# Layer norm of the depthwise convolution: two passes over the tiles, or one with shifted sums

## The chip, the cores and the metric

The kernel runs on one core of one Trainium2 chip, all in one program. The time is the device time of an execution in microseconds (us); less is better.

## The reference, cut to what matters

The whole is a chain of residual blocks on a sequence of 256 tokens with 1024 features, in f32: a first part (mixer, cross attention, MLP), then a conformer convolution, a gated MLP, sparse attention and another gated MLP. The change lies in the convolution block alone:

```python
def layernorm(x, g, b):
    xf = x.astype(jnp.float32)
    mu = jnp.mean(xf, axis=-1, keepdims=True)
    var = jnp.mean(jnp.square(xf - mu), axis=-1, keepdims=True)
    y = (xf - mu) * lax.rsqrt(var + EPS_2)
    return (y * g.astype(jnp.float32) + b.astype(jnp.float32)).astype(x.dtype)

def conformer_conv(h, w_pw1, b_pw1, w_dw, b_dw, ln_g, ln_b, w_pw2, b_pw2):
    u = h @ w_pw1 + b_pw1
    a, gate = jnp.split(u, 2, axis=-1)
    u = a * jax.nn.sigmoid(gate)
    u = causal_dwconv_2(u, w_dw, b_dw)        # 31 taps for each channel
    u = jax.nn.silu(layernorm(u, ln_g, ln_b))
    return u @ w_pw2 + b_pw2
```

The norm is over the 1024 channels of each token.

## The kernel before, in words

All activations lie feature-major: a tile is 128 channels (partitions) by 256 tokens, and there are eight. The weights come as a stream of 512 KB chunks, loaded by SyncE's DMA queue into the ring `WR`, and are split in two for three products (high by high, high by low, low by high; lines L867 to L869): ScalarE makes the high half `WH` (L1232), VectorE the low half `WL` (L1477). Each engine has its program in its own order, fixed by hand; `sp.to(n)` puts the split of the chunks up to n at that place of an engine's program, and the engines meet at semaphores. `AHEAD` is 3 chunks.

The first matrix `pw1` has 16 output tiles, gates and values by turns. VectorE scales each (L1492), ScalarE applies the sigmoid (L1406), and VectorE multiplies the two into the padded tile `UPAD` (L1807). Then comes the depthwise convolution, two tiles at a time in four rounds p = 0 to 3. Of its 31 taps VectorE does 13 as partial sums in `CD` (`taps` on VectorE, L1823 to L1828) and TensorE 18, as products with diagonal matrices of 64 by 64 that GpSimd builds in `DG` (L1974); the results stand in PSUM (`big`). TensorE's `taps(p)` runs the 18 (L1164), waits for `part_done`, and adds `CD` through the identity (L1169). A round is followed on ScalarE by `conv_out(p)`, a copy of the two tiles to `CX` (L1398).

TensorE's order is: tiles of `pw1` 0 to 7, then `taps(0)`, tiles 8 to 11, `taps(1)`, feature sums of `CX` 0 and 1, tiles 12 to 15, `taps(2)`, sums 2 and 3, `taps(3)`, sums 4 to 7. A sum over features is a matmul with a matrix of ones in plain f32 (L1175), which leaves the sum in all partitions. VectorE turns it into the mean `MU` (L1854) and subtracts this from the eight tiles (L1856); ScalarE squares each (L1415), TensorE sums the squares (`sum_squares("ln")`, L875), ScalarE takes Ln and Exp to have 1/sqrt (L1249, L1250), VectorE multiplies (L1859), ScalarE applies Silu with gain and bias (L1419) and rounds the high half `YH` (L1422), GpSimd the low half `YL` (L1936). The next matrix `pw2` begins with all three.

A function of ScalarE needs a table that holds it, and a change of table is an instruction of its own; `preload_act_table_set` puts one at a chosen place (L1412).

Of the kernel before, what the change touches and what calls it, by code (L numbers as in the profile page):

```python
# [7 lines left out]
P = 128  # L8
T = 256
TT = T // P  # L10
D = 1024
KD = D // P
# [15 lines left out]
F32 = mybir.dt.float32  # L28
F32R = mybir.dt.float32r
ALU = mybir.AluOpType  # L30
ACT = mybir.ActivationFunctionType
# [66 lines left out]
def program(nc, x_d, mem_d, stream_d, vec_d, const_d, small_d, out_d):  # L98
    stack = ExitStack()
    with stack:  # L100
# [5 lines left out]
        def sem(name):  # L106
            if name not in sems:
                sems[name] = stack.enter_context(nc.semaphore(name))
            return sems[name]
# [5 lines left out]
        SQ = sb("SQ", [P, KD, T])  # L115
# [7 lines left out]
        LNV = sb("LNV", [P, T])  # L123
        RS = sb("RS", [P, T])
        RS2 = sb("RS2", [P, T])
        SSUM = sb("SSUM", [P, T])
        ONES = sb("ONES", [P, P])
        EPS = sb("EPS", [P, 2])
        RST = sb("RST", [P, TT])

        def group(specs):
# [31 lines left out]
        OS = QT  # L163

        B = group([("SG", [P, 2, T], F32), ("AT", [P, 2, T], F32), ("UP", [P, KD, T + CONV_W - 1], F32),
                   ("CX", [P, KD, T], F32), ("CD", [P, 2, 2, 2, T], F32), ("MU", [P, T], F32),
                   ("DG", [P, 2, PE_TAPS, 2, 64], F32)])
        SG, AT, UPAD, CX, CD, MU, DG = (B[n] for n in ("SG", "AT", "UP", "CX", "CD", "MU", "DG"))
        C = group([("GU", [P, 2, T], F32), ("UH", [P, 2, T], F32R), ("UL", [P, 2, T], F32R),
# [16 lines left out]
        big = stack.enter_context(nc.psum_tensor("big", [P, 4, 512], F32))  # L186
        mis = stack.enter_context(nc.psum_tensor("mis", [P, 2, 512], F32))
# [12 lines left out]
        def con(name, a=0, b=None):  # L200
            w = dict(CONSTS)[name]
            return CON[:, CCOL[name] + a:CCOL[name] + (w if b is None else b)]
# [22 lines left out]
        class Chain:  # L225
# [15 lines left out]
            def link(self, ins):  # L241
                self.eng.wait_ge(self.sem, self.add(ins))
# [614 lines left out]
        def _(pe):  # L857
# [22 lines left out]
            def sum_squares(name):  # L880
                for k in range(SQ_COUNT.get(name, 8)):
                    sum_square(name, k)
# [271 lines left out]
            def taps(p):  # L1154


                pe.wait_ge(sem("up_ready"), 2 * p + 2)
                pe.wait_ge(sem("diagonals"), p + 1)
                if p >= 2:
                    pe.wait_ge(sem("cx_whole"), 2 * p - 2)  # L1160
                halves = [(r, c, slice(64 * r, 64 * r + 64), slice(64 * c, 64 * c + 64)) for r in range(2) for c in range(2)]
                for i in range(PE_TAPS):
                    for r, c, rs, cs in halves:
                        pe.matmul(big[cs, 2 * (p % 2) + r, 0:T], DG[rs, p % 2, i, c, :], UPAD[rs, 2 * p + c, i:i + T],  # L1164
                                  start=i == 0, stop=False, skip_group_check=True)
                pe.wait_ge(sem("part_done"), 4 * p + 4)
                for a in range(2):
                    for r, c, rs, cs in halves:
                        ins = pe.matmul(big[cs, 2 * (p % 2) + r, 0:T], con("ident2")[rs], CD[rs, p % 2, c, a],  # L1169
                                        start=False, stop=a == 1, skip_group_check=True)  # L1170
                ins.then_inc(sem("taps_ps"), 1)

            def sum_features(j):
                pe.wait_ge(sem("cx_whole"), j + 1)
                return pe.matmul(mis[:, 1, 0:T], ONES[:, :], CX[:, j], start=j == 0, stop=j == KD - 1,  # L1175
                                 skip_group_check=True)

# [2 lines left out]
            for p in range(4):  # L1180
                if p < 3:
                    gated(2 * p + 2)
                    gated(2 * p + 3)
                taps(p)
                if p >= 1:
                    sum_features(2 * p - 2)
                    sum_features(2 * p - 1)
            sum_features(KD - 2)
            sum_features(KD - 1).then_inc(sem("mean_ps"), 1)
            sum_squares("ln")  # L1190
            for j in range(KD):
                tile(START["pw2"] + j, TILE["pw2"] + j, YH, YL, base=(yl_ready, Y_BASE["pw2"]) if j == 0 else None)

# [29 lines left out]
        def _(act):  # L1223
# [22 lines left out]
            def rstd(name, out):  # L1246
                act.wait_ge(nps_ready, NORM[name] + 1)
                e = EPS[:, int(NORM[name] > NORM["final"]):int(NORM[name] > NORM["final"]) + 1]
                link(act.activation(LNV[:, :], mis[:, 0, 0:T], ACT.Ln, bias=e, scale=1.0 / NORM_DIM.get(name, D)))  # L1249
                act.activation(out[:, :], LNV[:, :], ACT.Exp, scale=-0.5).then_inc(rstd_ready, 1)  # L1250
# [143 lines left out]

            def conv_out(p):
                act.wait_ge(sem("taps_ps"), p + 1)
                for r in range(2):
                    act.activation(CX[:, 2 * p + r], big[:, 2 * (p % 2) + r, 0:T], ACT.Copy).then_inc(sem("cx_whole"), 1)  # L1398

            C0 = START["pw1"]  # L1400
            sp.to(C0 + 1 + AHEAD)
# [1 line left out]
            for j in range(8):  # L1403
                sp.to(C0 + 2 * j + 1 + AHEAD)
                act.wait_ge(acc_free, TILE["pw1"] + 2 * j + 1)
                act.activation(SG[:, j % 2], SG[:, j % 2], ACT.Sigmoid,  # L1406
                               bias=vec("b_pw1", 2 * j)).then_inc(sem("gate_done"), 1)
                sp.to(C0 + 2 * j + 2 + AHEAD)
                if j % 2 == 1 and j >= 3:
                    conv_out((j - 3) // 2)  # L1410
            conv_out(3)
            act.preload_act_table_set("natural_log_exp_and_others")  # L1412
            for k in range(KD):
                act.wait_ge(sem("cx_centred"), k + 1)
                act.activation(SQ[:, k], CX[:, k], ACT.Square).then_inc(sq_ready, 1)  # L1415
            rstd("ln", RS2)
            for k in range(KD):
                act.wait_ge(gy_ready, GY_BASE["pw2"] + k + 1)
                silu = ch.add(act.activation(GY[:, k], GY[:, k], ACT.Silu, bias=vec("ln_b", k), scale=vec("ln_g", k)))  # L1419
# [50 lines left out]
        def _(dve):  # L1470
# [342 lines left out]
            def taps(p, first, stop):  # L1813

                for m in range(first, stop):
                    c, n = m // own, m % own
                    j, i = 2 * p + c, PE_TAPS + m % own
                    x, w, o = UPAD[:, j, i:i + T], vec("w_dw", CONV_W * j + i), CD[:, p % 2, c, n % 2]
                    if n == 0:
                        dve.wait_ge(sem("up_ready"), j + 1)  # L1820
                        if p >= 2:
                            dve.wait_ge(sem("taps_ps"), p - 1)
                        tapped[0] = ch.add(dve.tensor_scalar(o, x, w, vec("b_dw", j), ALU.mult, ALU.add))  # L1823
                    elif n == 1:
                        tapped[1] = ch.add(dve.tensor_scalar(o, x, w, None, ALU.mult))
                    else:
                        dve.wait_ge(dve_chain, tapped[n % 2])
                        ins = dve.scalar_tensor_tensor(o, x, w, o, ALU.mult, ALU.add)  # L1828
                        if n < own - 2:
                            tapped[n % 2] = ch.add(ins)  # L1830
                        else:
                            ins.then_inc(sem("part_done"), 1)

            for p in range(5):
                if p < 4:
                    gate_half(2 * p)
                if p >= 1:
                    taps(p - 1, 0, 3)
                if p < 4:
                    value_half(2 * p)  # L1840
                    gated(2 * p)
                if p >= 1:
                    taps(p - 1, 3, 6)
                if p < 4:
                    gate_half(2 * p + 1)
                if p >= 1:
                    taps(p - 1, 6, 9)
                if p < 4:
                    value_half(2 * p + 1)
                    gated(2 * p + 1)  # L1850
                if p >= 1:
                    taps(p - 1, 9, 2 * own)
            dve.wait_ge(sem("mean_ps"), 1)
            link(dve.tensor_scalar(MU[:, :], mis[:, 1, 0:T], 1.0 / D, None, ALU.mult))  # L1854
            for k in range(KD):
                dve.tensor_tensor(CX[:, k], CX[:, k], MU[:, :], ALU.subtract).then_inc(sem("cx_centred"), 1)  # L1856
            rstd_done("ln")
            for k in range(KD):
                dve.tensor_tensor(GY[:, k], CX[:, k], RS2[:, :], ALU.mult).then_inc(gy_ready, 1)  # L1859
            for j in range(KD):  # L1860
                used(START["pw2"] + j)
                t = TILE["pw2"] + j
                link(dve.scalar_tensor_tensor(X[:, j], acc[:, t % 2, 0:T], vec("b_pw2", j), X[:, j], ALU.add, ALU.add))
                dve.sem_inc(acc_free, 1)
                gx("ffn2_0", j)
                if j > 0:
                    add_square("ffn2_0", j - 1)
                sp.to(START["pw2"] + j + 1 + AHEAD)
# [276 lines left out]
```

## Time and profile before

| | |
|---|---|
| time, median of 3 runs | 1168.76 us (1169.74, 1165.75, 1168.76) |
| profiled execution, its own time | 1165.05 us |
| its span in the profile | 1163.2 us |
| granted TensorE clock, mean over the span | 0.977 of full speed |
| TensorE matmuls busy | 1088.1 us, 94% |
| VectorE busy | 786.2 us, 68% |
| ScalarE busy | 530.8 us, 46% |
| GpSimd busy | 166.4 us, 14% |

The span is the time between the first and the last instruction; what lies around it makes up the rest of the execution's time. Busy time is a sum over the span and says nothing of who waits for whom. In a timeline each row has a start, a length, an engine, a line of the kernel, the tile written and those read, how many instructions stand in the row (x), and in brackets how long the engine had been idle before it and what released it. PE is TensorE, PEld its weight load, DVE VectorE, ACT ScalarE, POOL GpSimd. A plain f32 matmul leaves two records. Matmuls overlap, so the length of one is more than its share of the time; the distance between starts is what it costs.

### The profile page before, as it was taken

What the parts mean: (1) busy time and instruction counts of PE and PEld (TensorE: products, weight loads), DVE (VectorE), ACT (ScalarE), POOL (GpSimd) and SP (SyncE); (2) the same over time, 40 slices, a digit from 0 to 9 for tenths busy, and PEclk for the clock granted to TensorE, in tenths of its full rate; (3) what the DMA queues carried; (4) which work ended last, traced back from release to release, by engine and by line L of the source; (5) the groups of instructions that cost most, each with busy time, mean ns of one, the idle gap of its engine ahead of it and who ended that gap; (6) DMA issues with size and microseconds to landing.
All of it is one profiled execution on the core that took longest, in us unless ns stands there. A gap on an engine that the chain in (4) does not pass through costs nothing.

```text
span 1163.2 us, 22985 instructions
## 1 busy us (share of the span) xinstructions
PE 1088.1 (94%) x8721; PEld 1030.3 (89%) x8721; DVE 786.2 (68%) x1314; ACT 530.8 (46%) x917; POOL 166.4 (14%) x180
## 2 busy tenths in 40 slices
PE   5999899889999989997999999988899999999997
PEld 4989569789999979776999999987888999999997
DVE  5866567575555568884777677658966657777675
ACT  5443265454444445126544444445535545444442
POOL 2020014031111115112310100120010021100100
PEclk9999799899999999998999999989999999999999
DMA  8553214256566643321456555553630025655551
GB/s 309 156 166 100 59 51 132 96 157 186 184 185 184 181 145 122 98 74 28 159 195 191 181 173 195 182 145 94 215 113 16 2 73 158 200 179 186 180 192 44
DMA packets 46437, 165.25 MB, mean 142 GB/s; under 512 B 5152, under 2 KB 6176, under 8 KB 46240
## 3 DMA queue, kind: packets, MB, share of 16 engines
q1 hardware_dynamic: 45216, 163.24, 44.4%
q10 hardware_dynamic: 1152, 1.05, 0.4%
q8 instruction: 49, 0.80, 0.3%
q14 instruction: 20, 0.16, 0.0%
HBM read 162.17 MB, written 1.05 MB: 140 GB/s over the span
## 4 chain that ended last, share of the span: by engine, by line
PE 77%; DVE 15%; ACT 4%; issue 2%; POOL 1%; DMA 1%; SPq 0%; DVEq 0%; ACTq 0%
PE acc L867 14%; PE acc L869 14%; PE acc L868 14%; PE big L867 6%; PE big L869 6%; PE big L868 6%; DVE WL L1477 4%; DVE CD L1828 2%; PE mis L875 2%; PE acc L471 2%; PE big L442 1%; DVE G L1484 1%; PE acc L928 1%; PE acc L930 1%; PE acc L929 1%
## 5 line engine op out<-in xcount | busy, mean ns | idle before, releaser
L1477 DVE TENSOR_TENSOR WL<-WR,WH 128x1024 fp32r<-128x1024 f32 x302 | 370.6, 1239 | 152.9 <-ACT WH L1232 142.8
L867 PE MATMUL acc<-XH,WH 128*128 128x256 f32 x1392 | 406.1, 292 | 29.7 <-DVE WL L1477 13.3
L869 PE MATMUL acc<-XH,WL 128*128 128x256 f32 x1392 | 396.7, 285 | 0.0
L868 PE MATMUL acc<-XL,WH 128*128 128x256 f32 x1392 | 396.4, 285 | 0.0
L1232 ACT ACTIVATE WH<-WR 128x1024 fp32r<-128x1024 f32 x302 | 313.3, 1051 | 130.1 <-PE acc L869 90.5
L867 PEld LDWEIGHTS acc<-XH,WH 128*128 128x128 f32 x1392 | 269.5, 194 | 35.5 <-issue 20.1
L868 PEld LDWEIGHTS acc<-XL,WH 128*128 128x128 f32 x1392 | 269.3, 193 | 1.1
L869 PEld LDWEIGHTS acc<-XH,WL 128*128 128x128 f32 x1392 | 269.0, 193 | 0.0
L867 PE MATMUL big<-UH,WH 128*128 128x256 f32 x608 | 170.6, 281 | 0.3 <-POOL UL L1940 0.3
L868 PE MATMUL big<-UL,WH 128*128 128x256 f32 x608 | 169.7, 279 | 0.0
L869 PE MATMUL big<-UH,WL 128*128 128x256 f32 x608 | 169.7, 279 | 0.0
L1940 POOL TENSOR_TENSOR UL<-GU,UH 128x256 fp32r<-128x256 f32 x76 | 56.3, 741 | 493.4 <-ACT UH L1367 493.4
L867 PEld LDWEIGHTS big<-UH,WH 128*128 128x128 f32 x608 | 114.5, 188 | 0.5 <-POOL UL L1940 0.5
L869 PEld LDWEIGHTS big<-UH,WL 128*128 128x128 f32 x608 | 114.3, 188 | 0.0
L868 PEld LDWEIGHTS big<-UL,WH 128*128 128x128 f32 x608 | 114.1, 188 | 0.0
L1367 ACT ACTIVATE UH<-GU 128x256 fp32r<-128x256 f32 x76 | 31.8, 418 | 160.8 <-DVE GU L1746 86.8
L1932 POOL TENSOR_TENSOR XL<-G,XH 128x256 fp32r<-128x256 f32 x56 | 63.0, 1137 | 186.2 <-ACT XH L1239 186.2
L867 PE MATMUL acc<-YH,WH 128*128 128x256 f32 x256 | 76.1, 297 | 7.8 <-POOL YL L1936 6.4
L868 PE MATMUL acc<-YL,WH 128*128 128x256 f32 x256 | 73.4, 287 | 0.0
L869 PE MATMUL acc<-YH,WL 128*128 128x256 f32 x256 | 73.3, 286 | 0.0
L867 PEld LDWEIGHTS acc<-YH,WH 128*128 128x128 f32 x256 | 50.0, 195 | 10.6 <-issue 5.4
L868 PEld LDWEIGHTS acc<-YL,WH 128*128 128x128 f32 x256 | 50.2, 196 | 0.1
(296 smaller groups left out, 1341.1 us busy)
## 6 DMA issues: line engine op xcount, KB each, us to landing
WR<-weights SPq DMA_DIRECT2D x302, 512.0 KB, 3.6
X<-x_t SPq DMA_DIRECT2D x4, 256.0 KB, 6.3
MEM<-mem_t SPq DMA_DIRECT2D x1, 1024.0 KB, 10.1
result_t<-X SPq DMA_DIRECT2D x4, 256.0 KB, 2.2
CON<-constants SPq DMA_DIRECT2D x1, 896.0 KB, 12.3
CBUF<-KCV ACTq DMA_DIRECT2D x4, 128.0 KB, 5.5
CBUF<-KCV ACTq DMA_DIRECT2D x4, 127.5 KB, 6.3
SML<-small_weights SPq DMA_DIRECT2D x1, 480.0 KB, 14.2
```

Source lines behind the costliest of these rows:

```text
L442: pe.matmul(o[:, P:P + T], QP[:, j, P:T], k, start=False, stop=True, skip_group_check=True)
L471: ins = pe.matmul(acc[:, 0, (2 * br + tt) * P:(2 * br + tt) * P + P], PT[:, hh % 2, br, b * P:b * P + P], NV[:, m, 128 * g + 64 * br:128 * ...
L867: pe.matmul(out, wh, hi, start=start, stop=False, skip_group_check=True)
L868: pe.matmul(out, wh, lo, start=False, stop=False, skip_group_check=True)
L869: return pe.matmul(out, wl, hi, start=False, stop=stop, skip_group_check=True)
L875: ins = pe.matmul(mis[:, 0, 0:T], ONES[:, :], SQ[:, k], start=k == 0, stop=k == n - 1, skip_group_check=True)
L1232: act.activation(WH[:, cs % SPL], WR[:, cs % RAW], ACT.Copy).then_inc(w_high, 1)
L1367: act.activation(UH[:, us % 2], GU[:, us % 2], ACT.Copy).then_inc(u_high, 1)
L1477: dve.tensor_tensor(WL[:, cs % SPL], WR[:, cs % RAW], WH[:, cs % SPL].bitcast(F32), ALU.subtract).then_inc(w_low, 1)
L1828: ins = dve.scalar_tensor_tensor(o, x, w, o, ALU.mult, ALU.add)
L1932: pool.tensor_tensor(XL[:, k], G[:, k], XH[:, k].bitcast(F32), ALU.subtract).then_inc(xl_ready, 1)
L1940: pool.tensor_tensor(UL[:, us % 2], GU[:, us % 2], UH[:, us % 2].bitcast(F32), ALU.subtract).then_inc(sem("u_low"), 1)
```

## The change

The mean of the first 256 channels (tiles 0 and 1), called the shift here, is taken as soon as round 0 is in `CX`. It is subtracted from tiles 0 and 1 by VectorE, and from tiles 2 to 7 by one more group of identity matmuls in PSUM. From then on TensorE sums both the values and their squares as tiles come, and the variance is the mean of the squares less the square of the mean. Squares are taken straight from PSUM. Tiles are centred on VectorE behind the statistics, three ahead and the rest between the scalings.

```diff
@@ tiles
-                   ("CX", [P, KD, T], F32), ("CD", [P, 2, 2, 2, T], F32), ("MU", [P, T], F32),
+                   ("CX", [P, KD, T], F32), ("CD", [P, 2, 2, 2, T], F32), ("MU", [P, 3, T], F32),
@@ TensorE, taps(p)
+                if p == 1:
+                    for j in range(2):
+                        pe.wait_ge(sem("cx_whole"), j + 1)
+                        ins = pe.matmul(mis[:, 1, T:2 * T], ONES[:, :], CX[:, j], start=j == 0, stop=j == 1,
+                                        skip_group_check=True)
+                    ins.then_inc(sem("shift_ps"), 1)
                 pe.wait_ge(sem("part_done"), 4 * p + 4)
-                for a in range(2):
+                if p == 1:
+                    pe.wait_ge(sem("shift_done"), 1)
+                for a in range(2 if p == 0 else 3):
                     for r, c, rs, cs in halves:
-                        ins = pe.matmul(big[cs, 2 * (p % 2) + r, 0:T], con("ident2")[rs], CD[rs, p % 2, c, a],
-                                        start=False, stop=a == 1, skip_group_check=True)
+                        x = CD[rs, p % 2, c, a] if a < 2 else MU[rs, 0]
+                        ins = pe.matmul(big[cs, 2 * (p % 2) + r, 0:T], con("ident2")[rs], x, start=False,
+                                        stop=a == (1 if p == 0 else 2), skip_group_check=True)
@@ TensorE, sum_features(j): waits for cx_shifted (j < 2), cx_whole (j < 6) or cx_last
@@ TensorE, behind taps(p)
-                if p >= 1:
-                    sum_features(2 * p - 2)
-                    sum_features(2 * p - 1)
+                if p >= 2:
+                    for j in (2 * p - 4, 2 * p - 3):
+                        sum_features(j)
+                        sum_square("ln", j)
+            for j in (4, 5):
+                sum_features(j)
+                sum_square("ln", j)
             sum_features(KD - 2)
             sum_features(KD - 1).then_inc(sem("mean_ps"), 1)
-            sum_squares("ln")
+            for n, k in ((7, KD - 1), (8, KD - 2)):
+                pe.wait_ge(sq_ready, SQ_BASE["ln"] + n)
+                ins = pe.matmul(mis[:, 0, 0:T], ONES[:, :], SQ[:, k], start=False, stop=n == 8, skip_group_check=True)
+            ins.then_inc(nps_ready, 1)
@@ ScalarE, conv_out(p)
-                for r in range(2):
-                    act.activation(CX[:, 2 * p + r], big[:, 2 * (p % 2) + r, 0:T], ACT.Copy).then_inc(sem("cx_whole"), 1)
+                for r in range(2) if p < 3 else (1, 0):
+                    if p < 3:
+                        act.activation(CX[:, 2 * p + r], big[:, 2 * (p % 2) + r, 0:T], ACT.Copy).then_inc(sem("cx_whole"), 1)
+                    elif r == 0:
+                        act.wait_ge(sem("cx_last"), 1)
+                    if p > 0:
+                        act.activation(SQ[:, 2 * p + r], big[:, 2 * (p % 2) + r, 0:T], ACT.Square).then_inc(sq_ready, 1)
@@ ScalarE, in the loop over the gates, ahead of conv_out(1), and behind it
+                if j == 5:
+                    for r in range(2):
+                        act.wait_ge(sem("cx_shifted"), r + 1)
+                        act.activation(SQ[:, r], CX[:, r], ACT.Square).then_inc(sq_ready, 1)
...
+            act.preload_act_table_set("natural_log_exp_and_others")
             conv_out(3)
-            act.preload_act_table_set("natural_log_exp_and_others")
-            for k in range(KD):
-                act.wait_ge(sem("cx_centred"), k + 1)
-                act.activation(SQ[:, k], CX[:, k], ACT.Square).then_inc(sq_ready, 1)
-            rstd("ln", RS2)
+            act.wait_ge(sem("var_done"), 1)
+            link(act.activation(LNV[:, :], MU[:, 2], ACT.Ln, bias=EPS[:, 1:2]))
+            act.activation(RS2[:, :], LNV[:, :], ACT.Exp, scale=-0.5).then_inc(rstd_ready, 1)
@@ VectorE, behind its taps of round 1
+                if p == 2:
+                    dve.wait_ge(sem("shift_ps"), 1)
+                    dve.tensor_scalar(MU[:, 0], mis[:, 1, T:2 * T], -1.0 / (2 * P), None,
+                                      ALU.mult).then_inc(sem("shift_done"), 1)
+                    dve.wait_ge(sem("shift_done"), 1)
+                    for j in range(2):
+                        dve.tensor_tensor(CX[:, j], CX[:, j], MU[:, 0], ALU.add).then_inc(sem("cx_shifted"), 1)
@@ VectorE, behind all taps
+            dve.wait_ge(sem("taps_ps"), 4)
+            for r in range(2):
+                if r == 1:
+                    dve.wait_ge(sq_ready, SQ_BASE["ln"] + 7)
+                dve.tensor_copy(CX[:, 6 + r], big[:, 2 + r, 0:T]).then_inc(sem("cx_last"), 1)
             dve.wait_ge(sem("mean_ps"), 1)
-            link(dve.tensor_scalar(MU[:, :], mis[:, 1, 0:T], 1.0 / D, None, ALU.mult))
-            for k in range(KD):
-                dve.tensor_tensor(CX[:, k], CX[:, k], MU[:, :], ALU.subtract).then_inc(sem("cx_centred"), 1)
+            link(dve.tensor_scalar(MU[:, 1], mis[:, 1, 0:T], 1.0 / D, None, ALU.mult))
+            link(dve.tensor_tensor(MU[:, 0], MU[:, 1], MU[:, 1], ALU.mult))
+            dve.wait_ge(nps_ready, NORM["ln"] + 1)
+            dve.scalar_tensor_tensor(MU[:, 2], mis[:, 0, 0:T], 1.0 / D, MU[:, 0], ALU.mult,
+                                     ALU.subtract).then_inc(sem("var_done"), 1)
+            def centred(k):
...
+                return ch.add(dve.tensor_tensor(CX[:, k], CX[:, k], MU[:, 1], ALU.subtract))
+            left = [centred(k) for k in range(3)]
             rstd_done("ln")
             for k in range(KD):
+                dve.wait_ge(dve_chain, left[k])
                 dve.tensor_tensor(GY[:, k], CX[:, k], RS2[:, :], ALU.mult).then_inc(gy_ready, 1)
+                if k + 3 < KD:
+                    left.append(centred(k + 3))
```

## Rows read from the trace of the kernel before

**Rows 1.** The page, part 4: shares of the chain of waits.

```profile
PE 77%; DVE 15%; ACT 4%; issue 2%; POOL 1%; DMA 1%; SPq 0%; DVEq 0%; ACTq 0%
```

**Rows 2.** Timeline of TensorE, 494 to 535 us: start, length, engine, line.

```profile
494.28 1.09 PE L1169 MATMUL big<-CD,CON 64*64 64x256 f32 x16 [1.13 <-DVE CD L1828]
495.30 1.13 PE L1175 MATMUL mis<-CX,ONES 128*128 128x256 f32 x4
...
516.42 1.09 PE L1169 MATMUL big<-CD,CON 64*64 64x256 f32 x16 [0.54 <-DVE CD L1828]
...
518.50 8.01 PE L1164 MATMUL big<-UP,DG 64*64 64x256 f32 x144
...
526.29 0.64 PEld L1169 LDWEIGHTS big<-CD,CON 64*64 64x64 f32 x16 [0.25 <-DVE CD L1828]
...
527.32 1.99 PE L1175 MATMUL mis<-CX,ONES 128*128 128x256 f32 x8
530.74 3.72 PE L875 MATMUL mis<-SQ,ONES 128*128 128x256 f32 x16 [1.43 <-ACT SQ L1415]
```

**Rows 3.** Timeline of VectorE, 489 to 546 us.

```profile
489.79 4.43 DVE L1828 SCALAR_TENSOR_TENSOR CD<-UP,VEC,CD 128x256 f32<-128x256 f32 x11
499.35 0.42 DVE L1492 TENSOR_TENSOR SG<-acc,RS 128x256 f32<-128x256 f32 x1 [5.12 <-PE acc L869]
499.69 1.22 DVE L1477 TENSOR_TENSOR WL<-WR,WH 128x1024 fp32r<-128x1024 f32 x1
...
529.35 0.42 DVE L1854 TENSOR_SCALAR MU<-mis 128x256 f32<-128x256 f32 x1 [3.11 <-PE mis L1175]
529.81 2.77 DVE L1856 TENSOR_TENSOR CX<-CX,MU 128x256 f32<-128x256 f32 x8
...
545.13 0.48 DVE L1863 SCALAR_TENSOR_TENSOR X<-acc,VEC,X 128x256 f32<-128x256 f32 x1 [6.91 <-PE acc L869]
```

**Rows 4.** Timeline of ScalarE, 495 to 547 us.

```profile
495.44 0.66 ACT L1398 ACTIVATE CX<-big 128x256 f32<-128x256 f32 x2 [10.56 <-PE big L1169]
495.98 1.06 ACT L1232 ACTIVATE WH<-WR 128x1024 fp32r<-128x1024 f32 x1
...
534.50 0.47 ACT L1249 ACTIVATE LNV<-mis,EPS 128x256 f32<-128x256 f32 x1 [1.47 <-PE mis L875]
...
535.44 1.28 ACT L1419 ACT_TABLE_LOAD   x1
...
546.48 0.40 ACT L1240 ACTIVATE SQ<-X 128x256 f32<-128x256 f32 x1
```

**Rows 5.** Timeline of GpSimd (POOL), 495 to 545 us.

```profile
495.49 4.21 POOL L1974 TENSOR_TENSOR DG<-CON,VEC 128x1152 f32<-128x1152 f32 x2 [17.67 <-PE big L1169]
...
538.21 6.21 POOL L1936 TENSOR_TENSOR YL<-GY,YH 128x256 fp32r<-128x256 f32 x8 [38.52 <-ACT YH L1422]
```

**Rows 6.** Timeline of TensorE, the first products of `pw2`.

```profile
539.08 0.55 PE L867 MATMUL acc<-YH,WH 128*128 128x256 f32 x1 [4.62 <-POOL YL L1936]
...
540.17 0.42 PE L868 MATMUL acc<-YL,WH 128*128 128x256 f32 x1
540.39 0.41 PE L869 MATMUL acc<-YH,WL 128*128 128x256 f32 x1
...
544.70 0.28 PE L868 MATMUL acc<-YL,WH 128*128 128x256 f32 x1
544.82 0.28 PE L869 MATMUL acc<-YH,WL 128*128 128x256 f32 x1
```

**Rows 7.** Busy time by stretch; the third column from the end is the granted clock.

```profile
537.00:538.00 1.00, 0.00 (x0) 0.00 (x0) 1.00 (x4) 1.00 (x3) 0.00 (x0) 0.50 0.00 0
...
543.00:544.00 1.00, 1.00 (x5) 0.92 (x5) 0.00 (x0) 1.00 (x2) 1.00 (x2) 0.62 0.00 0
...
779.00:780.00 1.00, 1.00 (x8) 1.00 (x8) 0.00 (x0) 0.72 (x1) 0.00 (x0) 0.64 1.00 284
...
786.00:787.00 1.00, 1.00 (x10) 1.00 (x10) 1.00 (x2) 0.62 (x2) 0.00 (x0) 0.95 0.06 16
```

More of the change, by code:

```diff
@@ L1165, in taps @@
                                   start=i == 0, stop=False, skip_group_check=True)
+                if p == 1:
[4 more added lines that the diff above has]
+                    ins.then_inc(sem("shift_ps"), 1)
                 pe.wait_ge(sem("part_done"), 4 * p + 4)
-                for a in range(2):
+                if p == 1:
+                    pe.wait_ge(sem("shift_done"), 1)
+                for a in range(2 if p == 0 else 3):
                     for r, c, rs, cs in halves:
-                        ins = pe.matmul(big[cs, 2 * (p % 2) + r, 0:T], con("ident2")[rs], CD[rs, p % 2, c, a],
-                                        start=False, stop=a == 1, skip_group_check=True)
+                        x = CD[rs, p % 2, c, a] if a < 2 else MU[rs, 0]
+                        ins = pe.matmul(big[cs, 2 * (p % 2) + r, 0:T], con("ident2")[rs], x, start=False,
+                                        stop=a == (1 if p == 0 else 2), skip_group_check=True)
                 ins.then_inc(sem("taps_ps"), 1)
             def sum_features(j):
-                pe.wait_ge(sem("cx_whole"), j + 1)
+                if j < 2:
+                    pe.wait_ge(sem("cx_shifted"), j + 1)
+                elif j < 6:
+                    pe.wait_ge(sem("cx_whole"), j + 1)
+                else:
+                    pe.wait_ge(sem("cx_last"), j - 5)
                 return pe.matmul(mis[:, 1, 0:T], ONES[:, :], CX[:, j], start=j == 0, stop=j == KD - 1,
@@ L1852, in _ @@
                     taps(p - 1, 9, 2 * own)
-            dve.wait_ge(sem("mean_ps"), 1)
-            link(dve.tensor_scalar(MU[:, :], mis[:, 1, 0:T], 1.0 / D, None, ALU.mult))
-            for k in range(KD):
-                dve.tensor_tensor(CX[:, k], CX[:, k], MU[:, :], ALU.subtract).then_inc(sem("cx_centred"), 1)
+                if p == 2:
[10 more added lines that the diff above has]
+                dve.tensor_copy(CX[:, 6 + r], big[:, 2 + r, 0:T]).then_inc(sem("cx_last"), 1)
+            dve.wait_ge(sem("mean_ps"), 1)
+            link(dve.tensor_scalar(MU[:, 1], mis[:, 1, 0:T], 1.0 / D, None, ALU.mult))
[4 more added lines that the diff above has]
+            def centred(k):
+                if k < 6:
+                    dve.wait_ge(sem("cx_whole"), k + 1)
+                return ch.add(dve.tensor_tensor(CX[:, k], CX[:, k], MU[:, 1], ALU.subtract))
+            left = [centred(k) for k in range(3)]
             rstd_done("ln")
             for k in range(KD):
+                dve.wait_ge(dve_chain, left[k])
                 dve.tensor_tensor(GY[:, k], CX[:, k], RS2[:, :], ALU.mult).then_inc(gy_ready, 1)
+                if k + 3 < KD:
+                    left.append(centred(k + 3))
             for j in range(KD):
```

## The prediction

> **What bounds the kernel now.** I read the page first. 77% of the chain of waits is TensorE work [rows 1]: whatever adds TensorE time where TensorE sets the pace costs its full length, and whatever lands where another engine sets it costs nothing. The change touches only the convolution stage, some 457 to 545 us. There I read each engine's timeline, to see who is last at every hand-over.
>
> Call the four rounds p = 0 to 3. Each runs 144 small matmul records over the taps, then 16 that add VectorE's partial sums through an identity (L1169), which wait for VectorE. In round 1 TensorE stands 1.13 us before those [rows 2] and VectorE then idles 5.12 us until the next tile [rows 3]: slack on both sides, TensorE's at 493.2 to 494.3, VectorE's at 494.2 to 499.35. In round 2 TensorE waits again (0.54 us), so the start at 516.42 is VectorE's. In round 3 it doesn't wait; only its weight load does, for 0.25 us [rows 2]. So from 517.4 on TensorE is the pace, with at most 0.25 us of slack.
>
> Then the norm. TensorE sums the features to 529.31, VectorE makes the mean (0.42) and centres the first tile, ScalarE squares it, TensorE starts the squares at 530.74 and ends them at 534.46 [rows 2, 3, 4]. Ln starts at 534.50, the table load for Silu behind it runs from 535.44 to 536.72, and from there ScalarE and POOL pace all: Silu and high half of a tile, and POOL's low halves behind them in 6.21 us for 8, 0.78 a tile, to 544.42 [rows 4, 5]. The first product of the next matrix restarts at 539.08 and is fed at that pace [rows 6]. From 527.32 to the first Silu at 536.72, 9.4 us pass; that is all that this change can shorten, and ScalarE's part of it (from 534.50, 2.22 us) stays.
>
> **The change, part by part.**
>
> *Round 1 (shift).* Two more fp32 matmuls on TensorE between the taps and the identity adds. The taps end 1.13 before the adds' start at 494.28, at 493.15; two such matmuls take 1.13 (L1175 x4) [rows 2], so they end at 494.28, when VectorE's last tap (489.79 + 4.43 = 494.22) is also done. VectorE then writes the shift (as L1854, 0.42) to about 494.75 [rows 3], and TensorE's identity adds, which stand behind that wait with the weights product behind them, start at 494.8: 0.5 late. A third group of identity adds follows. One group is the half of 1.02 us (494.28 to 495.30) less the fill; I take 0.43, between 0.2 and 0.5. Taken away are two feature sums, 0.86 to 1.06. Sum: +0.5 +0.43 -0.86 = about +0.1 at the next tile, hence +0.1 for VectorE's restart at 499.35 and the whole of its unbroken work until 516.3. VectorE's two shifting adds (2 x 0.35, the pitch of L1856: 2.77 / 8) lie in its 5.12 us of idle time. ScalarE's squares of tiles 0 and 1 wait for them inside its 10.56 us of idle time before 495.44; the two squares among the copies put its next weight split (495.98) back by 0.9 for the later hand-over and 0.6 for the squares, to end near 498.6, while VectorE takes it at 499.69 [rows 3, 4]. That cover of about 1.1 us is the thinnest of the change: if it went, each 1 us over would go on VectorE's path. SP's queue and POOL's diagonals (4.21 us, from 496.4 to 500.6 instead of 495.49 to 499.7, wanted at 518.5) [rows 5] are not pushed past anything.
>
> *Round 2.* The identity adds start at 516.5. Third group +0.43. Then four sums stand where two stood. Four in a row take 1.99, two 1.13, so one more is 0.43; the eight squares in 3.72 give (3.72 - 1.99) / 4 = 0.43 as well [rows 2]. +0.86. The taps of round 3 start at 518.50 + 0.1 + 0.43 + 0.86 = 519.9, +1.4.
>
> *Round 3.* TensorE was at most 0.25 ahead of VectorE there; I take 0.15 as swallowed. Third group +0.43. The convolution is whole at 527.32 + 1.4 - 0.15 + 0.43 = 529.0, +1.7. ScalarE and VectorE then evacuate and square two tiles in turns (three or four steps of about 0.42, to 530.5), beside eight sums of older tiles (3.5 us, to 532.5): hidden. The table load moved ahead of this evacuation lies in the time in which ScalarE waits for round 3 (VectorE's and TensorE's work from 518.50 on): nothing.
>
> *The end of the sums.* Before, from 527.32: four sums, then mean, centring, first square (1.43 us of TensorE idle), eight sums, Ln at 534.50, that is 7.18 us. After: twelve sums without a break, 12 x 0.4325 + 0.3 = 5.49, to 534.5. The mean's own branch is as long: ten sums end at 529.0 + 4.33 + 0.3 = 533.6, mean 0.46, its square 0.46, 534.55. Then one new link, the variance on VectorE reading PSUM (0.48, L1863 [rows 3]) and a hand-over of 0.04: Ln at 535.1. Change: -1.7 for the gap and its hand-overs, +0.5 for the variance, so the +1.7 ends as +0.6.
>
> *Behind it.* Exp and the table load follow as before, so Silu starts at 537.35. VectorE now centres three tiles first (535.1 to 536.2), then alternates one scaled and one centred tile, 0.70 a pair: its first result is there at 536.65 under the table load, the second at 537.35, and from there it gives one per 0.70 against the 0.78 of ScalarE and POOL. Hidden, by 0.08 us a tile. The chain through POOL keeps its length. Net +0.6 us.
>
> **Ends of the unknown costs.** If the three identity groups cost only 0.2 each: -0.7, so -0.1. If each of the sums in a series that alternates between two output banks costs what a first one does (1.13 / 2 = 0.57, not 0.43): +0.14 x 14 = +2.0, so +2.6. I take the middle rows, since a row of eight in the same engine mode exists and the alternation has none: +0.6. The sum against the profiled execution is 1165.05 + 0.6 = 1165.7 (its span 1163.2 becomes 1163.8). But that execution is the fastest of the four shown; the runs beside it give 1165.75 to 1169.74, median 1168.76. I forecast the median: 1168.76 + 0.6 = 1169.4. This kernel's measurement can hardly tell less than 0.3%, 3.5 us, from no change.
>
> **Rivals.**
> 1. *A real gain.* The added sums and groups cost nothing before 529, because they fall where the taps are paced by VectorE. Then the convolution is whole at 527.4, sums end at 532.9, Ln at 533.5: -1.0, time 1167.8. For it: TensorE's weight load did wait for VectorE in round 3. Against it: for 0.25 us only, while 1.7 us are added. To gain over 3.5 us, more than a third of the 9.4 would have to vanish, and 5.5 of it are twelve sums. Chance 0.12.
> 2. *ScalarE's cover breaks in round 1 (or 2).* The added waits and squares hold the weight split back, VectorE idles, and its unbroken run to 516.3 moves. From the point where the split ends after 499.69, which is 1.1 us more than I count. A table load for a square between sigmoids (1.28 each way) would do it: 2.56 + 0.6 - 1.1 = +2.1, time 1170.9. Against it: under Silu's set the squares L1240 ran with no load between (546.48 after the load at 535.44) [rows 4]. Chance 0.10.
> 3. *Slower: the clock.* TensorE stood from 534.46 to 539.08 and its granted clock fell to 0.50 from about 537 to 543.4, that is from the 2.4 GHz level to 1.2 [rows 7]. It cost little, since ScalarE and POOL fed it at 0.78 a step. At the low level one matmul follows another by 0.22 us (540.17 to 540.39), at the high one by 0.12 (544.70 to 544.82) [rows 6], so a tile of 24 costs 2.4 us more. The standstill becomes 534.6 to 539.7, 0.5 longer. If the clock came back only 6.4 us behind the feed's end at 545, some 29 matmuls would be dear: 29 x 0.10 = 2.9, with +0.6 that is +3.5, time 1172.3 or more. That is the point from which it decides. For it: the same trace has a stretch with the engine busy throughout in which the clock was low from 779.6 to 786.05 [rows 7], some 6.4 us. Against it: behind the stand at 534 it came back 4.3 us after the restart, inside the fed tile. Chance 0.06.
>
> The Trainium skill, page "TensorE: Matmul & The Clock Gate", section "HAM oscillation — how this bites in real kernels", states that long pauses of the engine throttle its clock and that it has to be busy again before the clock is given back. By that rule this pause, being longer still, brings a dip in the changed kernel too. Here the trace agrees for the pause of 4.62 us [rows 6, 7]; the low stretch from 779.6, with the engine busy, is one that the rule doesn't explain.
>
> **How the numbers follow.** My forecast, -0.1 to +2.6, holds 0.68; rivals 0.12, 0.10 and 0.06; 0.04 for what I haven't seen. The runs of one kernel differ by 4 us here (a dip like that at 779.6 costs half its length, 3.2, and could be what comes and goes), so each case is blurred by about 2. Low end 1165.7: a median that catches the fast runs, 1165.75. High end 1172.2: the forecast with +2.6, and a slow draw, almost to rival 3. Faster by over 0.3%: 0.08, all of it from rival 1 and the draw. Slower by over 0.3%: 0.10, from rival 3 and half of the blur on rival 2. Within: 0.82.
>
> **What would show it.** Right: in the profile after, VectorE's restart near 499.4; round 3's taps start near 519.9; the identity adds of rounds 1 to 3 as 24 records, about 1.5 us each; twelve sums in a row in 5.5 us; Ln near 535.1; Silu near 537.4; the first matmul of the next matrix at 539.7. Wrong: the round 3 taps at 518.6 (rival 1); VectorE idle after 499.7 on a weight split, or a table load between sigmoids (rival 2); a granted clock of 0.50 past 546 (rival 3); sums with a pitch of more than 0.5 us, or VectorE late for a Silu.

## The result, and the profile after

The changed kernel takes 1170.74 us in the median of 22 runs (1163.97 to 1172.4); the kernel before, run beside it, 1167.24 us (22 runs, 1164.71 to 1170.13). The ratio is 1.0026, 95% interval 1.0015 to 1.0036: slower by 3.0 us, with 1.8 to 4.2 us as the bounds (the two medians as such lie 3.5 us apart). Forecast were 1169.4 us and +0.6 us over before.

Profiled executions wander by several us elsewhere, so I count inside one stretch, from ScalarE's first copy of round 0 (473.57 us before, 474.63 after: 1.06 of offset that the change has no part in) to VectorE's first residual (its first row `X<-acc` behind `pw2`). That length is called the stage here.

TensorE in the changed kernel, timeline, to hold against [rows 2] and [rows 6]:

```profile
494.14 1.13 PE L1170 MATMUL mis<-CX,ONES 128*128 128x256 f32 x4
495.88 1.09 PE L1179 MATMUL big<-CD,CON 64*64 64x256 f32 x16 [0.61 <-DVE MU L1886]
496.76 0.64 PE L1179 MATMUL big<-MU,CON 64*64 64x256 f32 x8
...
518.17 1.09 PE L1179 MATMUL big<-CD,CON 64*64 64x256 f32 x16 [1.13 <-DVE CD L1859]
...
521.55 8.00 PE L1164 MATMUL big<-UP,DG 64*64 64x256 f32 x144
529.38 1.04 PE L1179 MATMUL big<-CD,CON 64*64 64x256 f32 x16
530.24 0.61 PE L1179 MATMUL big<-MU,CON 64*64 64x256 f32 x8
530.78 0.70 PE L1190 MATMUL mis<-CX,ONES 128*128 128x256 f32 x2
...
535.20 1.03 PE L1212 MATMUL mis<-SQ,ONES 128*128 128x256 f32 x4
...
542.97 0.55 PE L867 MATMUL acc<-YH,WH 128*128 128x256 f32 x1 [6.74 <-POOL YL L1992]
```

The third identity group is the row of 8 records, 0.54 us from start to start in round 3 (530.24 to 530.78) with the refill behind it. The gap of 1.43 us in [rows 2] is gone, but the standstill ahead of the next matrix has grown from 4.62 to 6.74 us.

VectorE and ScalarE in the same kernel, against [rows 3] and [rows 4]:

```profile
495.31 0.42 DVE L1886 TENSOR_SCALAR MU<-mis 128x256 f32<-128x256 f32 x1
...
500.51 0.43 DVE L1523 TENSOR_TENSOR SG<-acc,RS 128x256 f32<-128x256 f32 x1 [3.98 <-PE acc L869]
500.85 1.95 DVE L1508 TENSOR_TENSOR WL<-WR,WH 128x1024 fp32r<-128x1024 f32 x1
...
541.15 1.09 DVE L1913 TENSOR_TENSOR GY<-CX,RS 128x256 f32<-128x256 f32 x3
548.67 0.48 DVE L1919 SCALAR_TENSOR_TENSOR X<-acc,VEC,X 128x256 f32<-128x256 f32 x1 [6.42 <-PE acc L869]
```

```profile
498.53 1.08 ACT L1255 ACTIVATE WH<-WR 128x1024 fp32r<-128x1024 f32 x1
...
536.80 0.51 ACT L1446 ACTIVATE LNV<-MU,EPS 128x256 f32<-128x256 f32 x1 [5.04 <-DVE MU L1901]
...
537.78 1.28 ACT L1450 ACT_TABLE_LOAD   x1
```

GpSimd, against [rows 5]; the last row is the first low half alone:

```profile
497.51 4.21 POOL L2030 TENSOR_TENSOR DG<-CON,VEC 128x1152 f32<-128x1152 f32 x2 [18.62 <-PE big L1179]
...
540.55 7.12 POOL L1992 TENSOR_TENSOR YL<-GY,YH 128x256 fp32r<-128x256 f32 x8 [38.84 <-ACT YH L1453]
...
540.55 2.28 POOL L1992 TENSOR_TENSOR YL<-GY,YH 128x256 fp32r<-128x256 f32 x1 [38.84 <-ACT YH L1453]
```

Two numbers stand out. The weight split at 500.85 takes 1.95 us, where its counterpart at 499.69 took 1.22, though its high half was ready (498.53 + 1.08). It ends at 502.80, 1.08 us after GpSimd's diagonals do (497.51 + 4.21 = 501.72). Before, the diagonals had ended at 499.70 (495.49 + 4.21) and the split began at 499.69: the two only just missed each other. And the first low half takes 2.28 us, where the eight took 6.21 together before: it starts at 540.55 amid VectorE's scalings and centrings and ends at 542.83, 0.59 us behind the last of them (541.15 + 1.09 = 542.24). Of its own work it has 0.73.

All kernels of this study, in us from the first copy of round 0 to the start of ScalarE's Ln, of its first Silu and of the first residual; ratios are to the kernel before:

| kernel | Ln | first Silu | first residual | time ratio (95%) |
|---|---|---|---|---|
| before | 60.93 | 63.16 | 71.56 | |
| changed | 62.17 | 64.44 | 74.04 | 1.0026 (1.0015 to 1.0036) |
| e1 | 62.34 | 64.61 | 73.99 | one execution |
| e2 | 62.18 | 64.45 | 73.22 | one execution |
| e3 (from before) | 62.06 | 64.29 | 72.70 | one execution |
| e4 | 62.18 | 64.45 | 73.76 | one execution |
| e5 | 59.34 | 61.61 | 70.92 | 0.9985 (0.9973 to 0.9997) |
| e6 | 58.74 | 61.01 | 69.49 | 0.9981 (0.9968 to 0.9994) |
| e7 (from before) | 60.33 | 62.57 | 70.61 | 1.0005 (0.9995 to 1.0016) |
| e8 | 58.75 | 61.02 | 68.74 | 0.9962 (0.9947 to 0.9977) |
| e9 | 62.18 | 64.46 | 72.93 | one execution |
| e10 (from before) | 60.34 | 62.57 | 70.30 | 0.9998 (0.9988 to 1.0008) |

Lengths up to Ln repeat well, so that one execution can be read to some hundredths of a us there: the four kernels with the same code up to Ln (changed, e2, e4, e9) have it at 62.17 or 62.18, e6 and e8 at 58.74 and 58.75, e7 and e10 at 60.33 and 60.34.

### The profile page after: what moved, and what is told of

It is laid out like the page before. It is cut to its first block, busy times and chain, and to the rows that moved or that the text cites. A ratio compares the mean times of both kernels' runs of the same rounds, so it can differ in the third digit from the quotient of the medians.

```text
span 1170.2 us, 23049 instructions
## 1 busy us (share of the span) xinstructions
PE 1092.6 (93%) x8749; PEld 1035.3 (88%) x8749; DVE 790.2 (68%) x1321; ACT 530.4 (45%) x915; POOL 167.8 (14%) x180
## 4 chain that ended last, share of the span: by engine, by line
PE 76%; DVE 16%; ACT 3%; issue 2%; POOL 1%; DMA 1%; SPq 0%; DVEq 0%; ACTq 0%
PE acc L867 14%; PE acc L869 14%; PE acc L868 14%; PE big L867 6%; PE big L869 6%; PE big L868 6%; DVE WL L1508 4%; DVE CD L1859 2%; PE mis L875 2%; PE acc L471 2%; PE big L442 1%; PE acc L928 1%; PE acc L929 1%; PE acc L930 1%; DVE G L1515 1%
```

## Experiments

**e1: diagonals earlier.**

```diff
+                ins.then_inc(sem("diag_read"), 1)      # TensorE, last product of the round with DG
-                    pool.wait_ge(sem("taps_ps"), p - 1)
+                    pool.wait_ge(sem("diag_read"), p - 1)
```

> The changed kernel, but GpSimd starts the diagonals of a round when TensorE's last product with the old ones has ended, and not when the whole round has. Stage length is counted from the first ScalarE copy of round 0 to the first residual on VectorE: 71.56 us before, 74.04 us changed. Theory (GpSimd and VectorE hold each other up when both read SBUF): the diagonals then end before VectorE splits its next weights, the split behind round 1's scaling takes 1.2 us and not 1.95, likewise the one behind round 0's (1.95 in both kernels), round 2's identity adds start 0.7 earlier, the stage is 0.7 to 1.5 us shorter (72.6 to 73.3). Rival (the split was long because ScalarE's high half or the load came late): both splits keep their 1.95 us and the stage its 74.0.

Measured: both splits short, the stage 73.99. The splits came as the theory had them, the gain did not. VectorE, ScalarE and GpSimd of this kernel show why:

```profile
477.01 1.21 DVE L1509 TENSOR_TENSOR WL<-WR,WH 128x1024 fp32r<-128x1024 f32 x1
...
494.31 0.42 DVE L1887 TENSOR_SCALAR MU<-mis 128x256 f32<-128x256 f32 x1 [0.62 <-PE mis L1171]
494.77 3.45 DVE L1891 TENSOR_TENSOR CX<-CX,MU 128x256 f32<-128x256 f32 x2
...
500.74 1.23 DVE L1509 TENSOR_TENSOR WL<-WR,WH 128x1024 fp32r<-128x1024 f32 x1 [0.80 <-ACT WH L1256]
```

```profile
498.25 0.42 ACT L1441 ACTIVATE SQ<-CX 128x256 f32<-128x256 f32 x1 [1.85 <-DVE CX L1891]
...
499.63 1.08 ACT L1256 ACTIVATE WH<-WR 128x1024 fp32r<-128x1024 f32 x1
```

```profile
493.32 4.61 POOL L2031 TENSOR_TENSOR DG<-CON,VEC 128x1152 f32<-128x1152 f32 x2 [16.84 <-PE big L1164]
```

The two shift additions on VectorE take 3.45 us instead of 0.76: they now stand inside GpSimd's work. ScalarE's square waits for them, its weight split comes late, and VectorE idles 0.80 us where the split had been 0.73 too long. What round 0's shorter split gained is already lost ahead of that: VectorE waits 0.62 us for TensorE's sum of the shift, and its first scaling of the next tile starts 25.87 us after the first copy (499.51), against 25.88 in the changed kernel. The collision moved; that is my second rival's chain (ScalarE's cover breaks), set off by GpSimd.

**e2: centring of tiles 3 to 7 left out** (part of the norm is not computed). The wait for those centrings goes too; the cut shows the work alone.

```diff
-                if k + 3 < KD:
-                    left.append(centred(k + 3))
```

> The changed kernel without the centring of tiles 3 to 7 (left out, so part of the norm is not computed): VectorE does eight scalings in a row and is done 1.7 us sooner. Theory: GpSimd's first low half, 2.28 us long in the changed kernel, takes 0.73 again, the first product of the next matrix starts 1.5 us earlier (about 4.0 us after the first Silu's start is 2.4 instead), and the stage is 1 to 2 us shorter than 74.04. Rival (the long first low half is GpSimd's own start, or the Silu chain is late because VectorE's alternation feeds it late): first low half stays above 1.5 us, stage within 0.3 of 74.0.

Measured: stage 73.22, 0.82 shorter; all eight low halves in 6.20 us, as before the change, while Silu starts where it did:

```profile
538.37 6.20 POOL L1990 TENSOR_TENSOR YL<-GY,YH 128x256 fp32r<-128x256 f32 x8 [38.84 <-ACT YH L1453]
```

The gain lies just under the 1 to 2 us expected. The first product stands 2.34 us after the first Silu, as in the kernel before (2.35), but the first residual 8.77 against 8.40. The 0.37 that are left go with the clock: it was granted at 0.50 until past 545.6, the end of the tile, where in the kernel before it rose inside the tile [rows 7].

**e3: the kernel before, diagonals later.**

```diff
-                    pool.wait_ge(sem("taps_ps"), p - 1)
+                    pool.wait_ge(sem("cx_whole"), 2 * (p - 1))
```

> The kernel before, with GpSimd's diagonals started only after ScalarE's two copies of the round, some 0.65 us later than before. Theory: now they overlap the weight split at 499.7 (1.22 us before), which grows to 1.7 to 1.95 us, and round 2's identity adds start 0.5 to 0.7 later; stage 71.56 + 0.6 = 72.1. Rival: the split keeps 1.22 us and the stage 71.56, since nobody waits for the diagonals.

Measured: 72.70, +1.14. GpSimd and VectorE in it:

```profile
475.44 4.20 POOL L1974 TENSOR_TENSOR DG<-CON,VEC 128x1152 f32<-128x1152 f32 x2 [21.94 <-ACT CX L1398]
...
498.00 4.20 POOL L1974 TENSOR_TENSOR DG<-CON,VEC 128x1152 f32<-128x1152 f32 x2 [18.36 <-ACT CX L1398]
```

```profile
478.08 2.64 DVE L1477 TENSOR_TENSOR WL<-WR,WH 128x1024 fp32r<-128x1024 f32 x1
...
501.51 1.77 DVE L1477 TENSOR_TENSOR WL<-WR,WH 128x1024 fp32r<-128x1024 f32 x1
```

Round 0 in the trace of the kernel before, GpSimd and VectorE:

```profile
473.62 4.20 POOL L1974 TENSOR_TENSOR DG<-CON,VEC 128x1152 f32<-128x1152 f32 x2 [21.24 <-PE big L1169]
```

```profile
476.95 1.95 DVE L1477 TENSOR_TENSOR WL<-WR,WH 128x1024 fp32r<-128x1024 f32 x1
```

Nobody waits for the diagonals, and still 0.69 us of delay in each round costs all of it in round 0 and 0.55 in round 1: round 1's split grows from 1.22 to 1.77, and round 0's, which had collided all along (1.95), to 2.64. I had counted round 1 alone. Each split ends 1.08 us after GpSimd's diagonals: at 503.28 behind 502.20, and at 480.72 behind 479.64.

**e4: the standstill filled.**

```diff
+            for i in range(12):
+                pe.matmul(big[:, i % 2, 0:T], ONES[:, :], SQ[:, 0], start=True, stop=True, skip_group_check=True)
```

> The changed kernel with twelve more fp32 matmuls of the size of a sum (into free PSUM, never read) behind the last sum of squares, so that TensorE works for 5.2 us of its 6.7 us standstill. If the clock is part of the loss: granted clock 1.00 throughout, the eight steps of the next matrix's first tile run at 0.36 us and are bound by GpSimd's low halves, the first residual comes 0.3 to 0.6 us earlier, stage 73.5 to 73.7. Rival (the clock costs nothing, since the feed is slower than TensorE at either level): stage 74.0, or longer if the fill holds the first product up.

Measured: 73.76, -0.28. By stretches (the granted clock is the third column from the end), the changed kernel first, then e4:

```profile
544.00:546.00 2.00, 2.00 (x10) 2.00 (x10) 0.00 (x0) 2.00 (x6) 2.00 (x4) 0.50 0.00 0
546.00:548.00 2.00, 2.00 (x10) 2.00 (x10) 0.00 (x0) 0.52 (x1) 1.67 (x3) 0.50 0.00 0
```

```profile
543.00:545.00 2.00, 1.86 (x10) 1.24 (x11) 0.00 (x0) 2.00 (x6) 2.00 (x4) 1.00 0.00 0
545.00:547.00 2.00, 1.78 (x10) 1.17 (x10) 0.00 (x0) 1.39 (x3) 2.00 (x4) 1.00 0.00 0
```

The clock stays at 2.4 GHz and the steps still come 0.69 us apart, at the rate of GpSimd's low halves. So in the changed kernel the clock is worth 0.3 us, no more: the low clock and GpSimd's pace are limits of nearly the same size.

**e5: the single pass without the shift.** The shift's matmuls, the third identity groups, VectorE's three shift instructions and the wait go; in their place:

```diff
                 if p == 1:
...
+                    for j in range(2):
+                        sum_features(j)
+                        sum_square("ln", j)
...
-                if p == 1:
-                    pe.wait_ge(sem("shift_done"), 1)
-                for a in range(2 if p == 0 else 3):
+                for a in range(2):
```

> The changed kernel without the shift: sums and squares are of the convolution as it is; the shift's two matmuls, the third identity group of rounds 1 to 3, VectorE's three shift instructions and the wait for them go, and the four sums of tiles 0 and 1 run in round 1 ahead of the identity adds. Stage (first copy of round 0 to first residual) 71.56 us before, 74.04 changed. Theory (the shift costs three groups of 0.43 and a wait of 0.5, and the single pass by itself saves the 1.43 us gap and two hand-overs): Ln comes 58.6 to 59.4 us after the first copy (60.93 before, 62.17 changed), the first Silu 2.3 later; GpSimd's long first low half stays, so the stage is 70.3 to 71.0 and the time 0.2% below before. Rival (the added length is the sums' own, alternating between two banks): Ln stays above 61, stage above 73.

Measured: 70.92, 3.12 shorter than the changed kernel; Ln at 59.34. In TensorE's timeline the four sums stand in round 1, where both kernels have it wait for VectorE, and the identity adds follow with no row for a wait:

```profile
493.65 0.59 PE L1182 MATMUL mis<-CX,ONES 128*128 128x256 f32 x2
494.08 0.59 PE L875 MATMUL mis<-SQ,ONES 128*128 128x256 f32 x2
494.61 1.10 PE L1173 MATMUL big<-CD,CON 64*64 64x256 f32 x16
```

The rival falls: sums that alternate between two banks start 0.43 us apart here too (493.65 to 494.08), and Ln is far below 61. The time, 0.9985, is 0.15% below before where 0.2% was expected. The first low half still takes 2.28 us in this kernel.

**e6: as e5, and GpSimd and VectorE apart.** The edit of e1, and VectorE does the low halves; GpSimd's are removed.

```diff
+            def low_half(k):
+                dve.wait_ge(yh_ready, Y_BASE["pw2"] + k + 1)
+                dve.tensor_tensor(YL[:, k], GY[:, k], YH[:, k].bitcast(F32), ALU.subtract).then_inc(yl_ready, 1)
...
+                if k >= 5:
+                    low_half(k - 5)
+            for k in range(3, KD):
+                low_half(k)
```

> As e5, with GpSimd and VectorE kept apart: the diagonals start when TensorE's last product with the old ones has ended (VectorE has no two-input work then, since the shift is gone), and VectorE takes the low halves of the eight tiles itself, behind its scalings, so that GpSimd has nothing there. Theory: no weight split of 1.95 us in the stage (0.7 less in each of rounds 0 and 1), Ln at 57.8 to 58.8 after the first copy, the first product of the next matrix 2.6 us after the first Silu, the last low half 7.0 after it; stage 69.0 to 70.0, bound in its last part by TensorE at the low clock. Time 0.2% to 0.4% below before. Rival (keeping them apart only moves the waits, as in e1): stage as in e5 within 0.3.

Measured: 69.49; no long split is left, Ln 0.60 earlier than in e5. The last part is bound by TensorE at the low clock, as expected: in this stretch it is busy throughout at a granted clock of 0.50, and VectorE and GpSimd are idle:

```profile
543.00:544.00 1.00, 1.00 (x6) 1.00 (x6) 0.00 (x0) 0.42 (x1) 0.00 (x0) 0.50 0.00 0
```

**e7: the kernel before, with the same two edits.**

> The kernel before (two passes), with GpSimd and VectorE kept apart in the same two places. Theory: the weight split behind round 0 takes 1.2 and not 1.95 us, everything from there to Silu comes 0.7 earlier (Ln at 60.2 after the first copy), the low halves on VectorE save another 0.3: stage 70.4 to 70.9 against 71.56, time 0.1% below before. If e7 gains as much as e6, the single pass gives nothing; if e6 is 1 us or more shorter in the stage, that is the single pass's own worth. Rival (no contention at all in the kernel before): 71.56.

Measured: 70.61, 0.95 shorter than before; the split behind round 0 takes 1.22 again:

```profile
476.67 1.22 DVE L1478 TENSOR_TENSOR WL<-WR,WH 128x1024 fp32r<-128x1024 f32 x1
```

The time doesn't show it: 1.0005, interval 0.9995 to 1.0016, where 0.9992 would be 0.95 us and lies outside the interval. Why is open (below). Against e6 the single pass without a shift is worth 1.12 us in the stage and 1.6 up to Ln.

**e8: e6 with the twelve filling matmuls.**

> As e6, with the twelve filling matmuls behind the last sum of squares. Theory (in e6 the first tile of the next matrix is bound by TensorE at its low clock, 0.695 us a step): with the clock at 1.00 the tile is bound by ScalarE's high halves, 0.80 a step from an earlier start, and the stage is 0.5 to 1.2 us shorter than e6's. Rival (ScalarE's pace hides the clock): same stage as e6 within 0.3.

Measured: 68.74, 0.75 less than e6; ratio 0.9962. TensorE and VectorE:

```profile
531.53 5.34 PE L1208 MATMUL big<-SQ,ONES 128*128 128x256 f32 x24
537.52 0.36 PE L867 MATMUL acc<-YH,WH 128*128 128x256 f32 x1 [0.65 <-DVE YL L1895]
...
540.44 0.39 PE L867 MATMUL acc<-YH,WH 128*128 128x256 f32 x1 [0.18 <-DVE YL L1895]
...
541.24 0.39 PE L867 MATMUL acc<-YH,WH 128*128 128x256 f32 x1 [0.18 <-DVE YL L1895]
```

```profile
542.26 0.48 DVE L1911 SCALAR_TENSOR_TENSOR X<-acc,VEC,X 128x256 f32<-128x256 f32 x1 [0.73 <-PE acc L869]
```

TensorE now waits 0.18 us for each of the last two low halves, which come 0.80 us apart, as ScalarE's high halves do (539.53, 540.33): the end of the stage is bound by ScalarE's pace. This version beats the kernel before, and by its ratio the changed one too.

**e9: the changed kernel, complete, low halves on VectorE** (e6's edit of the low halves alone).

> The changed kernel, complete, with the eight low halves ahead of the next matrix taken by VectorE behind its scalings and none by GpSimd; the diagonals and the shift stay. Theory (in the changed kernel GpSimd's first low half waited for VectorE's burst): Ln and Silu as in the changed kernel (62.2 and 64.4 after the first copy of round 0), the first product about 3.2 us after the first Silu instead of 3.9, the first residual 8.5 after it instead of 9.6; stage 72.9 to 73.2. Rival (only GpSimd's own rate of 0.73 a tile is in question and ScalarE is ahead of it anyway): stage within 0.3 of 74.0.

Measured: 72.93, 1.11 shorter, with Ln and Silu where they were. The first product stands 2.98 us after the first Silu, against 3.90. The rest of the gain lies behind it, where the steps come 0.64 us apart instead of 0.69:

```profile
541.12 0.55 PE L867 MATMUL acc<-YH,WH 128*128 128x256 f32 x1 [5.83 <-DVE YL L1911]
```

**e10: the kernel before with all of e8 but the single pass.**

> The kernel before (two passes) with all that e8 has beside the single pass: diagonals started early, low halves on VectorE, twelve filling matmuls behind the sum of squares. Theory (the single pass without the shift is worth 1.5 us of e8's 2.8 in the stage: Ln 60.33 in e7, 58.75 in e8): Ln at 60.3, stage 70.1 to 70.4, time between before and e8, about 0.1% below before. Rival (e8 gains by the clock alone): stage within 0.4 of e8's 68.74, time as e8's.

Measured: 70.30, time 0.9998 (0.9988 to 1.0008), where about 0.1% less was expected. The single pass without the shift is worth 1.56 us in the stage, all of it ahead of Silu: from the first Silu to the first residual e8 takes 7.72 us and e10 7.73. The filling matmuls are a little too many here. The first product follows them without a wait, 2.56 us after the first Silu and not 2.00 as in e7; TensorE makes that up before the tile ends. The intervals of e8 and e10 don't touch, so the gain in time is real; their quotient, 0.9964, is some 4 us with an uncertainty of 2, more than the stage shows (below).

## Why the prediction was right, and where it was short

The time lay in the range and within 0.3%, as the likeliest case had it, but the move is 3.0 us and not 0.6. That the time itself came within 1.4 us of the forecast is in part luck: the kernel before, in 22 runs, has a median 1.5 us below that of the three runs I started from, which hid about half of the error. By its own steps, each in us of the stage:

- *Round 1.* VectorE's restart was put 0.1 late: 25.88 against 25.78 us after the first copy, +0.10. Right. The cover called the thinnest, ScalarE's split, held: 499.61 against VectorE's 500.85.
- *"POOL's diagonals ... are not pushed past anything."* Wrong, and the step that failed. They start with the hand-over of round 1, 0.9 us later by my own count (measured 0.96), and I asked only who waits for them. They ran into the weight split: +0.73. e3 makes a loss of the same kind in the kernel before by moving the diagonals alone; e1 and e6 have no long split. The term could have been read from the trace of the kernel before: round 0's split of 1.95 us, shown with e3, is the same collision.
- *Round 2.* Third group and two more sums were put at +1.29. The round 3 taps start at 46.92 against 44.93, +1.99, of which 0.69 was there at the identity adds of round 2 (43.54 against 42.85): 1.30. Right. (The 0.83 of round 1 had become 0.69 by then: in the kernel before, VectorE paused for 0.12 us ahead of its scaling at 505.11, 1.31 us behind the start of the three taps before it; in the changed one these are 1.19 apart.)
- *Round 3.* I let 0.15 be swallowed by the wait for VectorE; none was (identity adds at 54.75 against 52.76, +1.99 too): TensorE had been the later one there already. The convolution was whole at +2.40 (56.15 against 53.75), not +1.7.
- *The end of the sums.* 5.49 + 0.5 + 0.04 was forecast from there to Ln; it took 6.02 (530.78 to 536.80). Right. So Ln came 1.24 late, not 0.6.
- *Behind it.* "The chain through POOL keeps its length": wrong. I checked that VectorE's alternation keeps ahead of ScalarE, and it did, but not what it does to GpSimd beside it. Silu to first residual took 9.60 against 8.40: +1.20. e2 gives back 0.82 of it by shortening VectorE's burst, and what is left, 0.37, goes with the clock; e4 puts 0.28 on the clock directly. e9 gives back 1.11 by leaving GpSimd nothing to do there.
- *The clock rival* named a real term, 0.3 us in the changed kernel (e4) and 0.75 in e6 (e8), but not at the size that decides. Its sign, a granted clock of 0.50 past 546, did come: the clock was low to about 548.4. But the low halves themselves came until 547.67 (540.55 + 7.12), so it outlasted them by 0.7 us, and not by the 6.4 that the rival needed. The sign was badly chosen. The 6.4 were misread too: the stretch of the kernel before was low from about 779.3, since 0.64 granted over 779 to 780 is 0.72 us at 0.50 [rows 7], so it lasted some 6.7.

The sum in the stage, as measured: 0.10 + 0.73 - 0.14 in round 1, +1.30 in round 2, +0.41 for round 3's group, -1.16 for the sums' end, +0.04 up to Silu, +1.20 behind = 2.48 us. The interval of the time, 1.8 to 4.2 us, holds it.

The profiled spans differ by 7.0 us, not 2.5. From ScalarE's table load at 764.87 (768.39 after) to its last rounding of an activation, in code that is the same, the changed kernel's execution took 391.25 us against 387.80, another 3.45. Two stretches of it, before first, then changed:

```profile
830.00:850.00 20.00, 17.42 (x130) 16.07 (x129) 17.79 (x33) 8.59 (x16) 3.61 (x5) 1.00 0.32 108
850.00:870.00 20.00, 17.68 (x97) 14.61 (x96) 13.03 (x21) 7.52 (x13) 3.08 (x4) 1.00 0.44 130
```

```profile
830.00:850.00 20.00, 17.43 (x119) 16.12 (x118) 17.54 (x33) 8.59 (x16) 3.62 (x4) 0.91 0.44 142
850.00:870.00 20.00, 17.68 (x87) 14.59 (x86) 11.73 (x22) 8.00 (x15) 3.44 (x4) 0.83 0.34 100
```

The granted clock fell for parts of these stretches in the one execution and not in the other; over the same code the twelve profiled executions of this study take from 387.8 to 391.3 us. Whether some kernels draw these dips more often than others is open; it could be why e7 and e10 show less in the time than in the stage, and e8 more.

## What to carry to other kernels

When a hand-over moves, ask of every instruction that moves with it not only who waits for it, but what it will run beside. An engine that nobody waits for can still hold another up. Look for such a pair in the trace of before first: one instruction that takes different times in different places is the sign. Here the single pass alone gives 1.6 us of the stage (e8 against e10), and the shift, meant for the accuracy of the difference of two means, cost 3.1 (e5). How accurate the variance is without it on data with a large mean, no run here shows.

## What the runs showed of the hardware

GpSimd and VectorE exclude each other in instructions that both read two operands from SBUF. A split of 1.22 us took 1.95, 1.77 and 2.64 beside diagonals that still had 0.87, 0.69 and 1.56 us to run, and every time it ended 1.08 us behind them, as if it had begun when they ended. The diagonals kept their 4.20 or 4.21 us, so this is no sharing at half the rate. In e1 two additions of 0.76 together took 3.45: the first 1.18, done between GpSimd's two instructions, the second 2.34. VectorE's shift in the same kernel, with one operand and that in PSUM, ran in its 0.42 us (from 494.31) beside the diagonals.

It holds the other way round. A low half of 0.73 took 2.28 beside VectorE's burst; VectorE's stream had no gap, and GpSimd did not get in between its instructions. The kernel before shows the same outside the stage, already in part 5 of its page: GpSimd's subtraction of one size takes 741 ns in the mean where it is `UL`, and 1137 ns where it is `XL`.

```profile
L1940 POOL TENSOR_TENSOR UL<-GU,UH 128x256 fp32r<-128x256 f32 x76 | 56.3, 741 | 493.4 <-ACT UH L1367 493.4
L1932 POOL TENSOR_TENSOR XL<-G,XH 128x256 fp32r<-128x256 f32 x56 | 63.0, 1137 | 186.2 <-ACT XH L1239 186.2
```

One such `XL` and the weight split of VectorE beside it; the split had 0.94 us to run (to 553.35) when `XL` began, and `XL` took 0.80 more than 0.74:

```profile
552.13 1.22 DVE L1477 TENSOR_TENSOR WL<-WR,WH 128x1024 fp32r<-128x1024 f32 x1
```

```profile
552.41 1.54 POOL L1932 TENSOR_TENSOR XL<-G,XH 128x256 fp32r<-128x256 f32 x1 [1.69 <-ACT XH L1239]
```

The Trainium skill, page "SBUF — State Buffer", section "SBUF: two separate sides", states this rule: the two engines share a pair of ports under an exclusive lock, a VectorE instruction with two SBUF inputs takes it against a GpSimd instruction that reads SBUF, and the later one waits in full. All the durations above agree with it. I had not weighed it, and worked out from [rows 3] and [rows 5] it would have given the missing 0.73: 4.21 us from 496.4 end at 500.6, 0.8 into a split that starts at 499.8.
